# Row one-hots of the gate stage: from GpSimd and VectorE to two passes on ScalarE, and VectorE's gate program written out

## The reference, cut to what matters

```python
def peer_ffn(h, wq, sub_keys, u_tab, v_tab):          # 16384 experts = 128 x 128 keys, 8 heads, top 16
    ...
    idx = jnp.take_along_axis(cand_i, pos, axis=-1)    # i * 128 + j of the chosen experts
    gate = jax.nn.softmax(best, axis=-1)
    ...
    def block(args):
        xt, it, gt = args
        a = jax.nn.gelu(jnp.einsum('td,tkd->tk', xt, u_tab[it]))
        return jnp.einsum('tk,tkd->td', gt * a, v_tab[it])
```

## Time and profile before

| what | value |
|---|---|
| median of 3 runs | 2294.5 us (2293.08 to 2297.16) |
| profiled execution | 2292.26 us, span 2290.5 us |
| PE busy | 2173.6 us, 95% of the span |
| DVE / ACT / POOL busy | 1438.7 / 623.6 / 796.5 us |
| chain that ended last, by engine | PE 78%, POOL 9%, DVE 5%, DMA 3% |
| chain that ended last, by line | L965 30%, L906 19%, POOL eB L1855 6%, POOL ugat L1824 3% |

### The profile page before, as it was taken

One profiled execution on the slowest core, in us unless ns is written; L12 is line 12 of the kernel. 1 busy time (PEld: TensorE's weight loads), 2 busy tenths in 40 slices (PEclk: granted clock), 3 DMA queues, 4 the chain that ended last, 5 costly groups with the idle time before them and its releaser, 6 DMA issues.

```text
span 2290.5 us, 30680 instructions
## 1 busy us (share of the span) xinstructions
PE 2173.6 (95%) x9868; PEld 1665.6 (73%) x9868; DVE 1438.7 (63%) x3055; ACT 623.6 (27%) x930; POOL 796.5 (35%) x713
## 2 busy tenths in 40 slices
PE   7999998798989999999999898999999999999998
PEld 3554444546987877877777787787888888888886
DVE  4221426334889998878777787324766666666665
ACT  2111012333222223333333233223323222222222
POOL 0000001003225554998989898001222212121220
PEclk7999999898999999999999999999999999999999
DMA  9122124204204444699997899855988888888883
GB/s 338 45 74 72 44 85 181 97 33 160 75 1 153 144 139 138 205 301 309 297 282 250 270 298 288 254 174 210 352 285 294 285 291 289 289 288 290 288 289 146
DMA packets 293477, 475.54 MB, mean 208 GB/s; under 512 B 148871, under 2 KB 150055, under 8 KB 292872
## 3 DMA queue, kind: packets, MB, share of 16 engines
q1 hardware_dynamic: 256520, 340.20, 45.1%
q0 software_dynamic: 36864, 134.23, 16.6%
HBM read 401.76 MB, written 72.61 MB: 207 GB/s over the span
## 4 chain that ended last, share of the span: by engine, by line
PE 78%; POOL 9%; DVE 5%; DMA 3%; issue 2%; SPq 2%; ACT 1%; DVEq 0%; ACTq 0%; POOLq 0%
PE ps L965 30%; PE ps L906 19%; POOL eB L1855 6%; PE ps L624 5%; PE ps L717 3%; PE ps L843 3%; POOL ugat L1824 3%; PE ps L878 3%; PE ps L879 3%; PE ps L683 2%; PE ps L946 2%; SPq L521 2%; PE ps L623 1%; DMA uraw<-in_u_t 1%; PE ps L666 1%
## 5 line engine op out<-in xcount | busy, mean ns | idle before, releaser
L906 PE MATMUL ps<-h2hi,uhi 128*128 128x512 f32 x1024 | 449.8, 439 | 20.3 <-DVE scores L1375 7.7
L906 PE MATMUL ps<-h2hi,ulo 128*128 128x512 f32 x1024 | 404.9, 395 | 0.0
L965 PE MATMUL ps<-vhi,whi 128*128 128x512 f32 x1024 | 399.2, 390 | 5.6 <-DVE wlo L1475 5.6
L906 PE MATMUL ps<-h2lo,uhi 128*128 128x512 f32 x1024 | 403.7, 394 | 0.0
L965 PE MATMUL ps<-vhi,wlo 128*128 128x512 f32 x1024 | 399.1, 390 | 0.0
L965 PE MATMUL ps<-vlo,whi 128*128 128x512 f32 x1024 | 399.0, 390 | 0.0
L1832 POOL DMA_INDIRECT vgat<-in_v_tab,idx x128 | 145.4, 1136 | 660.0 <-DVE y L1485 508.3
L1855 POOL TENSOR_SCALAR eB<-iota,jcur 128x128 f32<-128x128 f32 x384 | 318.1, 841 | 18.8 <-DVE jcur L1440 17.0
L1473 DVE TENSOR_TENSOR vlo<-vraw,vhi 128x1024 fp32r<-128x1024 f32 x128 | 156.8, 1225 | 216.6 <-ACT vhi L1748 216.6
L1748 ACT ACTIVATE vhi<-vraw 128x1024 fp32r<-128x1024 f32 x128 | 135.5, 1061 | 465.8 <-PE ps L965 464.0
L946 PEld LDWEIGHTS ps<-eA,eB 128*128 128x128 f32 x1024 | 192.2, 191 | 93.0 <-POOL eB L1855 25.6
(11 more groups left out here) (270 smaller groups left out, 2993.7 us busy)
## 6 DMA issues: line engine op xcount, KB each, us to landing
uraw<-in_u_t SPq DMA_DIRECT2D x128, 512.0 KB
vraw<-in_v_tab SPq DMA_DIRECT2D x128, 512.0 KB
gelu_scratch<-aout SPq DMA_DIRECT2D x128, 256.0 KB
gate_scratch<-gst SPq DMA_DIRECT2D x16, 2048.0 KB, 14.9
ain<-gelu_scratch SPq DMA_DIRECT2D x128, 256.0 KB, 4.1
gin<-gate_scratch SPq DMA_DIRECT2D x128, 256.0 KB, 4.4
wring<-in_w_ada SPq DMA_DIRECT2D x12, 2048.0 KB, 10.6
wring<-in_w_in SPq DMA_DIRECT2D x6, 2048.0 KB, 8.5
```

The source lines that it names most:

```text
L906: last = pe.matmul(ps[:, b % 4, :], w[:, b % 2, k, :], h[:, k, LP:T], start=(k == 0 and j == 0), stop=(k == KD - 1 and j == 2))
L965: last = pe.matmul(ps[:, y_bank(t) + h, :], w[:, b, (t - 1) * P:t * P], v[:, b, h * 512:(h + 1) * 512], start=(start and j == 0), stop=(st ...
```

## The change

GpSimd and VectorE no longer make `eB`. ScalarE makes it for a whole block of eight tokens in `slot_keys`: eight passes Abs(j - iota) over 128 columns, each with the token's column of `cols_hk` as its bias, a wait until they are done, and one pass Relu(1 - x) over all 1024 columns in place. That gives exactly 1 where j equals iota and 0 elsewhere. `slot_keys(n + 1)` stands behind `uhi` of block n + 1 and ahead of the `gst` copies of block n; `slot_keys(0)` stands in block 39 ahead of `uhi` of block 40. TensorE waits once for each block for `eB`. VectorE reads `cols_hk` in place of `cur`; `cur`, `jcur` and their semaphores go, and the gate programs of VectorE and ScalarE are written out over all four rounds with no loop. GpSimd's gate program keeps the gathers alone. The diff, with its core:

```diff
@@ gate_matrix (TensorE)
-                        if not dve_row(q):
-                            pe.wait_ge(onehot_j_ready, (it * NB_B + b) * POOL_ROWS + k - k // 4 + 1)
+                        if k == 0:
+                            pe.wait_ge(onehot_j_ready, it * NB_B + b + 1)
@@ VectorE
-            def step_b(it, first):
-                if not first:
-                    dve.wait_ge(onehot_j_ready, it * POOL_ROWS * NB_B)
-                    dve.wait_ge(onehot_ready, it * P)
-                dd = bass.ds(it * P, P)
-                dve.tensor_copy(jcur[:], cols_hk[:, 1, dd]).then_inc(jcur_ready, 1)
-                dve.tensor_copy(cur[:], cols_hk[:, :, dd]).then_inc(cur_ready, 1)
-                dve.wait_ge(cur_ready, it + 1)
...
-                        if dve_row(q):
-                            dve.tensor_scalar(eB[:, b % 2, k], iota[:], cur[:, 1, q:q + 1], None, ALU.is_equal)
...
-            loop(dve, NTD, step_b)
+            for n in range(BLK_A, BLK_C):
+                m = n - BLK_A
+                for k in range(TB):
+                    q = TB * m + k
+                    if q >= RING:
+                        dve.wait_ge(onehot_used, q + 1 - RING)
+                    dve.tensor_scalar(eA[:, q % RING], iota[:], cols_hk[:, 0, q:q + 1], cols_hk[:, 2, q:q + 1],
+                                      ALU.is_equal, ALU.mult).then_inc(onehot_ready, 1)
+                    if k == 4:
+                        split_u(n + 1, n + 1)
...
@@ ScalarE
+            def slot_keys(m):
+
+                act.wait_ge(cl_drained, m // NB_B + 1)
+                if m >= 2:
+                    act.wait_ge(onehot_used, TB * (m - 1))
+                for k in range(TB):
+                    q = TB * m + k
+                    last = act.activation(eB[:, m % 2, k], iota[:], ACT.Abs, bias=cols_hk[:, 1, q:q + 1], scale=-1.0)
+                seq(last)
+                act.activation(eB[:, m % 2], eB[:, m % 2], ACT.Relu, bias=1.0, scale=-1.0).then_inc(onehot_j_ready, 1)
...
+                if n == BLK_A - 1:
+                    slot_keys(0)
                 pair(n, n % 4, False, False)
...
+                    if n + 1 < BLK_C:
+                        slot_keys(n + 1 - BLK_A)
                     stage(it, b, first)
                     gelu(n, b, False)
-            step_b(0, True, False)
-            step_b(1, False, True)
-            with act.Fori(2, NTD) as it:
-                step_b(it, False, False)
+            for it in range(NTD):
+                step_b(it, it == 0, it == 1)
@@ GpSimd
-                if b == 0:
-                    pool.wait_ge(jcur_ready, it + 1)
-                if n >= 2:
-                    pool.wait_ge(onehot_used, TB * (n - 1))
-                for k in range(TB):
-                    if not dve_row(TB * b + k):
-                        pool.tensor_scalar(eB[:, b % 2, k], iota[:], jcur[:, TB * b + k:TB * b + k + 1], None, ALU.is_equal
-                                           ).then_inc(onehot_j_ready, 1)
                 if n:
                     for e in range(DOTS_B):
                         gather_u(DOTS_B * (n - 1) + e + GSLOT)
```

More of the change, by code:

```diff
@@ L71 @@
 T_EARLY = 4
-POOL_ROWS = TB - TB // 4
 CAND = [(0, 2, 16), (2, 2, 8), (4, 4, 4), (8, 8, 2)]
 NCAND = sum(na * nb for _, na, nb in CAND)
-def dve_row(q):
-    return q % 4 == 3
 MIX_ORDER = [("mix", 0), ("mix", 1), ("mix", 2), ("turn", 0), ("mix", 3), ("turn", 1), ("mix", 4), ("turn", 2),
@@ L174, in bass_hybrid_layer @@
         eB = at("eB", 126, [P, 2, TB, 128])
-        cur = at("cur", 134, [P, 3, 128])
-        jcur = at("jcur", 136, [P, 128])
         gst = at("gst", 139, [P, 2, 128, 64])
@@ L398, in bass_hybrid_layer @@
         dot_done = sem("dot_done")
-        cur_ready = sem("cur_ready")
         dots_gelu = sem("dots_gelu")
@@ L420, in bass_hybrid_layer @@
         onehot_used = sem("onehot_used")
-        jcur_ready = sem("jcur_ready")
         gate_full = sem("gate_full")
@@ L1417, in split_u, with dot @@
                 dve.tensor_tensor(ulo[:, b % 2], uraw[:, b % 4], uhi[:, b % 2].bitcast(F32), ALU.subtract).then_inc(ulo_ready, 1)
[L1419 to L1426, removed]
+            def dot(g):
+                r, k = g // DOTS_IT, g % DOTS_IT
+                if k == 0 and r:
+                    dve.wait_ge(dots_gelu, r)
+                if g:
+                    dve.wait_ge(dot_done, g)
+                dve.wait_ge(u_gathered[g % GSLOT], 16 * (g // GSLOT + 1))
+                dve.tensor_tensor_reduce(junk[:], ugat[:, g % GSLOT], h2row[:], 1.0, 0.0, ALU.mult, ALU.add,
@@ L1427, in dot, with slot_weights @@
                                          dots[:, k:k + 1]).then_inc(dot_done, 1)
-            def slot_weights(it):
-                hk = bass.ds(it * DOTS_IT, DOTS_IT)
-                dve.wait_ge(dots_gelu, it + 1)
+            def slot_weights(r):
+                hk = slice(r * DOTS_IT, (r + 1) * DOTS_IT)
+                dve.wait_ge(dots_gelu, r + 1)
                 dve.tensor_tensor(w0[:, hk], acur[:], gate0[:, hk], ALU.mult).then_inc(w0_ready, 1)
-            def step_b(it, first):
-                if not first:
-                    dve.wait_ge(onehot_j_ready, it * POOL_ROWS * NB_B)
-                    dve.wait_ge(onehot_ready, it * P)
-                dd = bass.ds(it * P, P)
-                dve.tensor_copy(jcur[:], cols_hk[:, 1, dd]).then_inc(jcur_ready, 1)
-                dve.tensor_copy(cur[:], cols_hk[:, :, dd]).then_inc(cur_ready, 1)
-                dve.wait_ge(cur_ready, it + 1)
-                for b in range(NB_B):
-                    n = it * NB_B + b + BLK_A
-                    for k in range(TB):
[L1446 to L1449, removed]
-                        if dve_row(q):
-                            dve.tensor_scalar(eB[:, b % 2, k], iota[:], cur[:, 1, q:q + 1], None, ALU.is_equal)
[L1452 to L1459, removed]
@@ L1461, in _ @@
-            loop(dve, NTD, step_b)
+            for n in range(BLK_A, BLK_C):
[8 more added lines that the diff above has]
+                        split_u(n + 1, n + 1)
+                if m % NB_B == 2 and m >= NB_B:
+                    slot_weights(m // NB_B - 1)
+                for e in range(DOTS_B):
+                    dot(DOTS_B * m + e)
@@ L1847, in _ @@
             for n in range(NTD * NB_B):
-                it, b = n // NB_B, n % NB_B
-                if b == 0:
-                    pool.wait_ge(jcur_ready, it + 1)
-                if n >= 2:
-                    pool.wait_ge(onehot_used, TB * (n - 1))
-                for k in range(TB):
-                    if not dve_row(TB * b + k):
-                        pool.tensor_scalar(eB[:, b % 2, k], iota[:], jcur[:, TB * b + k:TB * b + k + 1], None, ALU.is_equal
-                                           ).then_inc(onehot_j_ready, 1)
                 if n:
```

## The result

The changed kernel takes 2309.97 us (median of 9 runs, 2301.73 to 2314.84) against 2293.08 us for the kernel before (9 runs, 2288.62 to 2297.42). The ratio is 1.0076, with a 95% interval of 1.0056 to 1.0096. The forecast of 2271 and its range of 2256 to 2298 both miss it.

The account below looks back on a forecast made before the run. TensorE was taken as the bound, the gate stage losing 53.1 us to its pace. From 2292.26 us, -5.4 (between bursts) -46.9 + 26.6 (bursts) -0.5 + 2.8 (start) gave 2268.9; as a median 2271, range 2256 to 2298.

Parts of the forecast that it names:

- What bounds the kernel: Gate stage: 522.6 us against 469.4 at TensorE's pace; 53.1 us lost, mainly to late `uraw` and GpSimd's `eB`.
- The cost of lateness: Gate-stage bursts: `uraw` needed about 31.8 us after the burst's opening block ends; beyond its lateness a burst loses 2.4 us.
- e7: Start of a burst's count: end of the block behind which the first `gst` store goes out.
- What goes, GpSimd's `eB`: Between bursts: without `eB` GpSimd is busy 2.4 us a block, so the 5.4 us lost there go.
- e12: End of a burst's count: end of the fifth block after e7; five blocks at TensorE's pace take 36.7 us.
- What moves, the gathers: Seven bursts: 8 gathers in each, `uraw` landing at 33.2 us, so 26.6 us lost in place of 46.9.
- What goes, the round's start: VectorE's loop return in rounds 2 and 3: stalls of 3.34 and 2.79 us go, counted as no gain of their own.
- ScalarE's passes: Gate stage: making `eB` takes 3.5 us, ScalarE's block 6.1 us against TensorE's 7.335, so it costs nothing.
- The start: Block 40: `slot_keys(0)` waits for `cols_hk` ahead of `uhi`, losing 2.8 us in place of 0.5.
- (a): Rival, chance 0.22: the gate-stage bursts stay at about 7 us each, 49 in place of 46.9, giving 2293 us.
- (c): Rival, chance 0.10 with its table form: ScalarE becomes the bound; Abs at 0.52 us gives 2309, table loads 2334.
- (d): Rival, 0.08 if large or something else slow: written-out VectorE and ScalarE programs wait for instructions, 1 to 3 us a round.

Follow-up runs that it names:

- held to the third: Changed kernel with each pair of gathers held until TensorE has used the third one-hot of the next block: 2290.56 us, ratio 0.9986.
- before with spread stores: Kernel before the change with each half of `gst` stored in eight 512 KB parts instead of two of 2048 KB: 2264.8 us, ratio 0.9873.
- the run with one column copy: Changed kernel with VectorE's gate program as a loop with its column copy again, one-hots staying with ScalarE: 2313.72 us, ratio 1.0091.

## Why the prediction was wrong, by its own steps

The forecast misses by 39.0 us in the medians and by 45.7 in the profiled executions. 36.3 of the 45.7 lie in the stage (535.5 against 499.2): 32.7 in the bursts, 3.0 outside them, 0.6 in the first block. The rest lies outside it, nearly all in code ahead of the change.

- **What bounds the kernel** held. The loss is that of late `uraw` and of GpSimd; with GpSimd relieved and the bursts gone the stage runs at TensorE's pace.
- **The cost of lateness** held: a need at 31.8 us after e7 and 2.4 us for the restart were forecast; with that need the seven bursts of after have 2.1 to 2.5, the 63 a median of 2.2.
- **What goes, GpSimd's `eB`** held: 7.33 us between bursts, from the second block behind e12 on. Of the 5.4 us, though, 3.3 came back in the first block behind e12, which takes 7.3 to 8.2 us. One reading is slightly off: 384 x 841 ns and 124 x 1198 ns are 471.5 us; the 466.7 is the sum of the two busy times, in which passes overlap. Nothing hangs on it.
- **What moves, the gathers: this step failed**, and it carries most of the miss: 59.3 us in place of 26.6, since `uraw` landed at 37.8 us on average and not at 33.2. It took the number of gathers issued between e7 and the landing as the measure, and found 8, 9 and 10 with landings of 33.2 to 39.4. The count after the change was right, 8. But the measure counts issues up to the landing, not what the transfers serve ahead of the load. The bursts of before with 9 and 10 had 8 up to the load's issue, like every burst of after, and one or two behind it, as in the seventh, where the last goes out at 1409.17 and the load at 1403.42; the second had 6. The gathers behind the load, which the change takes away, were worth little: from issue to landing the load takes 6.7 us in after, 6.7 in the kernel held to the third, which still has two of them, and 7.6 in before.

  In the second burst of before, which set the 33.2, only 4.8 gathers were served before the load went out; in after it is 8.0 to 8.6 in each burst, since the pair issued just before e7 is served inside it. The sentence that this pair goes out "when the transfers have room" is the wrong one. It goes out 2.2 to 4.4 us ahead of the first gate store and takes the first 7 us from it.

  By the line above (1.43), 1.9 more served than before's mean of 6.2 are 2.7 us of a later load, and 2.6 were measured (31.1 against 28.5); both kernels are in that line, so this is no independent check. What is shown by an edit is that the issue time does it: the pair moved 5 us later gives 22 of the 59 us back.

  One landing was also read low: the fifth burst of before has `uraw` at 40.2 us after e7 (1281.13 - 1240.96), not 39.4. That makes "2 us for a gather" looser still.
- **What goes, the round's start** held in after: nothing of its own. With the loop back, 17.3 us for its two bursts are as much as two others (17.1), and the ratios to before (1.0091 and 1.0076) lie in each other's intervals. In before, writing the program out shortened the stage by 7.5 us, with a time that can't be told from 0. Where the bursts are gone the stall is bare: before with spread stores has it in its blocks of 12.06 and 12.98 us.
- **ScalarE's passes** held. The step is 2.44 / 8 = 0.305 us (forecast 0.28), one takes 394 ns (387), the pass over 1024 columns 1.06; ScalarE still waits 1.39 us a block for TensorE ahead of a `gst` copy. No table load was added.
- **The start** held in its mechanism and its size, 1.25 to 2.8 us against 2.8 less 0.5.
- **The rivals.** (a), the bursts stay, named the right place with a price of 7 us, and its reason, that the bursts cheap in before were entered late, fits the list of costs: the second, third and sixth rose from 3.1, 4.7 and 5.4 us to 9.0, 9.7 and 7.6. They grew to 8.5 on average, which is 10 us beyond its 2293. But entering at full pace is not enough for 8.5: held to the third they cost 5.3. That they could grow by the change itself was in no rival. (c) gave 2309, which is the time measured, by a mechanism that is not there: in the 470 us above ScalarE is busy for 372 (79%) and the blocks still lie 7.33 us apart. Its number is a coincidence. (d): nothing in after shows such waits over 0.8 us on VectorE.

The prediction named its own test: landing at 36 us or more with 8 gathers. That is what came.

## What to carry to other kernels

An engine that is relieved does its next duty earlier, and if that duty is issuing transfers, they move against everything that shares the DMA engines: ask where they land relative to the largest bunch of stores, not only how many there are. Count the transfers served ahead of the issue of the one that matters, with those already pending when the bunch begins, not those issued before it lands. And where a bunch of stores holds an in-order queue, spread the stores first: here that alone gave 1.3% to before and made the change worth 0.9% (2264.8 to 2244.5) where it cost 0.8% without.

## What the runs showed of the hardware

- How many small pieces of a store pass beside gathers of large ones depends on when the gathers are issued: 81 to 101 small packets in the first 7 us beside some 240 of gathers with the pair at -0.3 and 1.0 us, against 1653 to 2186 beside as many with it at -3.0 and -1.5. The Trainium skill ("DMA: Bandwidth & Descriptors", Queues, rings and completion order) has each DMA engine take turns between queues by whole packets of some 9 to 17 descriptors. By this rule a turn of gathered pieces moves many times the bytes of a turn of 256-byte pieces; the trace agrees in direction (1.05 MB against 0.13 MB of small pieces in after's 7 us). Why 0.6 and 1.3 us of issue time decide so much of it no run here shows.
- The same gather instruction holds GpSimd for 0.93 to 2.05 us; in the gate stage 1.40 on average in after and 1.20 in before.
- VectorE's jump back to the start of its loop costs 1.90 to 2.25 us of idle time in the run with one column copy, 2.79 and 3.34 in before. The Trainium skill ("Runtime: NRT & Kernel Launch", Instruction fetch mechanics) names the mechanism, a taken branch whose target has to be fetched; the trace shows an idle time without a releaser and can't name its cause.
- An Abs with a column as bias and a Relu(1 - x) run between gelus without a table load: 576 such passes, no load more.
- Behind the waits of after's bursts, 5.5 to 7.1 us each, the granted clock was 0.5 (1.2 GHz) every time; behind the 1.2 us in the second and third burst of before it stayed at 1.00.
